# Weight terms of two output projections: formed on POOL in SBUF, or by adding transfers in DRAM

## The reference

```
y = concat([ya, yb, ym]) * silu(z)        # 512 x 1024
x = x + y @ w_out                         # w_out: 1024 x 1024, float32
```

## Time and profile before

| | us |
|---|---|
| median of 3 runs | 1134.42 |
| lowest and highest run | 1134.27, 1134.92 |
| profiled execution, its own time | 1134.12 |
| its span, first to last instruction | 1132.3 |
| PE busy | 1126.3 |
| DVE, ACT, POOL busy | 724.7, 614.6, 197.0 |

### The profile page before, as it was taken

One profiled execution on the slowest core, in us unless ns is written; L12 is line 12 of the kernel. 1 busy time (PEld: TensorE's weight loads), 2 busy tenths in 40 slices (PEclk: granted clock), 3 DMA queues, 4 the chain that ended last, 5 costly groups with the idle time before them and its releaser, 6 DMA issues.

```text
span 1132.3 us, 15715 instructions
## 1 busy us (share of the span) xinstructions
PE 1126.3 (99%) x6090; PEld 935.0 (83%) x6090; DVE 724.7 (64%) x1222; ACT 614.6 (54%) x1062; POOL 197.0 (17%) x193
## 2 busy tenths in 40 slices
PE   9999999999999999999999999999999999999998
PEld 7888888888888888888889888777888888877877
DVE  5584534599845776534558667667786575666786
ACT  5533431243436676634246677777545587577752
POOL 1000135440000000000000002643503000706530
PEclk9999999999999999999999999999999999999999
DMA  6423476673331212233255523231254233222431
GB/s 195 133 75 112 124 247 233 218 244 100 122 112 57 93 58 73 76 127 112 75 204 156 130 86 76 74 92 58 95 186 132 76 111 104 75 75 76 147 124 74
DMA packets 115026, 134.13 MB, mean 118 GB/s; under 512 B 18620, under 2 KB 93756, under 8 KB 113416
## 3 DMA queue, kind: packets, MB, share of 16 engines
q1 hardware_dynamic: 113720, 128.93, 35.9%
q10 hardware_dynamic: 1232, 4.19, 1.0%
HBM read 120.37 MB, written 12.74 MB: 118 GB/s over the span
## 4 chain that ended last, share of the span: by engine, by line
PE 98%; ACT 1%; DMA 0%; DVE 0%; issue 0%; DVEq 0%; ACTq 0%
PE acc L2052 22%; PE acc L2053 22%; PE acc L2054 22%; PE aux L2052 3%; PE aux L2054 3%; PE aux L2053 3%; PE aux L2538 3%; PE aux L2526 3%; PE acc L2502 3%; PE acc L2451 2%; PE acc L2453 2%; PE acc L2452 2%; PE aux L2284 1%; PE aux L2286 1%; PE aux L2285 1%; PE aux L2144 1%
## 5 line engine op out<-in xcount | busy, mean ns | idle before, releaser
L2052 PE MATMUL acc<-ht_hi,whi 128*128 128x512 f32 x712 | 278.1, 391 | 0.0
L2054 PE MATMUL acc<-ht_hi,wlo 128*128 128x512 f32 x712 | 277.1, 389 | 0.0
L2053 PE MATMUL acc<-ht_lo,whi 128*128 128x512 f32 x712 | 277.1, 389 | 0.0
L1406 DVE TENSOR_TENSOR wlo<-raw,whi 128x2048 fp32r<-128x2048 f32 x68 | 159.5, 2346 | 101.8 <-ACT whi L951 95.6
L951 ACT ACTIVATE whi<-raw 128x2048 fp32r<-128x2048 f32 x68 | 129.9, 1910 | 56.8 <-DMA raw<-w_in_dram 22.1
L2052 PEld LDWEIGHTS acc<-ht_hi,whi 128*128 128x128 f32 x712 | 133.7, 188 | 28.1 <-DVE wlo L1406 0.6
L2054 PEld LDWEIGHTS acc<-ht_hi,wlo 128*128 128x128 f32 x712 | 133.6, 188 | 27.9
L2053 PEld LDWEIGHTS acc<-ht_lo,whi 128*128 128x128 f32 x712 | 133.7, 188 | 27.1
L848 POOL TENSOR_SCALAR whi<-raw 128x512 fp32r<-128x512 f32 x52 | 39.5, 760 | 621.9 <-DMA raw<-e_w_in_dram 464.6
L2052 PE MATMUL acc<-whi,ht_hi 128*128 128x512 f32 (+1 forms) x224 | 83.9, 375 | 0.0
L2054 PE MATMUL acc<-whi,ht_lo 128*128 128x512 f32 (+1 forms) x224 | 83.8, 374 | 0.0
(11 more groups left out here) (344 smaller groups left out, 2160.5 us busy)
## 6 DMA issues: line engine op xcount, KB each, us to landing
raw<-w_in_dram SPq DMA_DIRECT2D x72, 512.0 KB, 4.6
raw<-o_w_in_dram SPq DMA_DIRECT2D x28, 512.0 KB, 4.7
weight_terms<-term_parts SPq DMA_DIRECT2D x8, 1024.0 KB, 4.8
raw<-e_w_in_dram SPq DMA_DIRECT2D x14, 512.0 KB, 5.2
raw<-w_proj_pool_dram SPq DMA_DIRECT2D x8, 512.0 KB, 4.0
term_parts<-o_w_out_dram SPq DMA_DIRECT2D x8, 512.0 KB, 6.4
raw<-w_proj_mlstm_dram SPq DMA_DIRECT2D x8, 512.0 KB, 4.1
raw<-w_out_dram SPq DMA_DIRECT2D x8, 512.0 KB, 4.4
```

The lines of the kernel that those rows point to most:

```text
L1406: v.tensor_tensor(wlo[:, slot, :], raw[:, slot, :], whi[:, slot, :].bitcast(F32), ALU.subtract).then_inc(w_split, 1)
L2052: mm(out_, w_hi_, x_hi, start=first, stop=False)
L2053: mm(out_, w_hi_, x_lo, start=False, stop=False)
L2054: return mm(out_, w_lo_, x_hi, start=False, stop=last)
```

## The change

The strips, POOL's subtractions and SP's 27 DMAs for them are gone, with the buffer `term_parts`. In their place POOL issues DMAs from DRAM to DRAM: 14 for the first layer and 8 for the second. For each layer four blocks are copied into the terms' places, two blocks are added to two of them, then T1 is added to T2, and T2 to T4; a wait stands between the steps. POOL begins once the eighth tile of transposed x is split (`tr_lo`). SP no longer does anything for the terms between weight loads, and waits for the last add (`fourth_added`) where it waited for the stores. The terms are now sums without a minus sign; the signs are taken up by the half sums and by the additions into the rows.

```diff
-            between_loads(0)
-            for u in range(4):
-                load(wview(A["w_proj_pool"][0]), u * UC, plan["pa"][0] + u)
-                between_loads(1 + u)
+            stage("pa", wview(A["w_proj_pool"][0]), 0)
...
                 load(W1, u * UC + COL_QK, plan["qk"][0] + u)
-                between_loads(5 + u)
...
-                    for landed in terms_out:
-                        sp.wait_ge(landed, 8 * len(BATCHES))
+                    sp.wait_ge(fourth_added, 32)
...
-            for b in range(len(BATCHES)):
-                pool.wait_ge(parts_in[b % 2], 16 * sum(PARTS[b % 2:b + 1:2]))
-                b11, b12, b21, b22 = (term_parts[:, b % 2, q, :] for q in range(4))
-                step(nc.gpsimd.tensor_tensor(b11, b12, b11, ALU.subtract))
-                step(nc.gpsimd.tensor_tensor(b12, b22, b12, ALU.subtract))
-                step(nc.gpsimd.tensor_tensor(b22, b22, b11, ALU.subtract))
-                nc.gpsimd.tensor_tensor(b21, b21, b22, ALU.subtract).then_inc(terms_made, 1)
+            def block(L, row, col):
+
+                view, cols = wview(A["eo"[L] + "_w_out_2"][0]), slice(WIDE * col, WIDE * col + WIDE)
+                if L or row:
+                    return [(slice(0, P), slice(0, 4), view[:, 4 * row:4 * row + 4, cols])]
+                halves_ = A["e_w_out_2"][0][0:3 * P].rearrange("(e k p) n -> e p k n", e=2, p=HD2)
+                return [(slice(HD2 * e, HD2 * e + HD2), slice(0, 3), halves_[e, :, :, cols]) for e in range(2)] + \
+                    [(slice(0, P), slice(3, 4), view[:, 3:4, cols])]
+
+            def weight_sums(L):
+                copied = blocks_copied_of(L)
+                for q, (row, col) in ((T1, (0, 0)), (T3, (0, 1)), (T2, (1, 1)), (T4, (1, 0))):
+                    for rows, ks, view in block(L, row, col):
+                        pool.dma_start(terms_dram[L, q][rows, ks, :], view).then_inc(blocks_copied, 16)
+                pool.wait_ge(blocks_copied, copied)
+                for q, (row, col) in ((T1, (0, 1)), (T3, (1, 1))):
+                    for rows, ks, view in block(L, row, col):
+                        pool.dma_start(terms_dram[L, q][rows, ks, :], view, accum_op=ALU.add).then_inc(pairs_added, 16)
+                pool.wait_ge(pairs_added, pairs_added_of(L))
+                pool.dma_start(terms_dram[L, T2], terms_dram[L, T1], accum_op=ALU.add, max_dma_last_dim=4 * WIDE).then_inc(third_added, 16)
+                pool.wait_ge(third_added, 16 * (L + 1))
+                pool.dma_start(terms_dram[L, T4], terms_dram[L, T2], accum_op=ALU.add, max_dma_last_dim=4 * WIDE).then_inc(fourth_added, 16)
...
+            for L in range(2):
+                if L == 0:
+                    pool.wait_ge(tr_lo, KT)
+                weight_sums(L)
...
-                        ins = v.tensor_tensor(sum_raw[:, k, :], y_tile(L, k)[:, UC:S], y_tile(L, k + 4)[:, UC:S], ALU.add)
+                        ins = v.tensor_tensor(sum_raw[:, k, :], y_tile(L, k + 4)[:, UC:S], y_tile(L, k)[:, UC:S], ALU.subtract)
...
-                        ins = v.tensor_tensor(sum_less[L][:, k, :], sum_raw[:, k, :], y_tile(L, k)[:, 0:UC], ALU.subtract)
+                        ins = v.scalar_tensor_tensor(sum_less[L][:, k, :], sum_raw[:, k, :], -1.0, y_tile(L, k)[:, 0:UC],
+                                                     ALU.mult, ALU.subtract)
...
-                    return v.tensor_tensor(rows, bank, rows, ALU.add)
+                    return v.tensor_tensor(rows, rows, bank, ALU.subtract if half else ALU.add)
...
-                        ins = v.tensor_tensor(sum_less[L][:, k, :], y_tile(L, k + 4)[:, 0:UC], sum_less[L][:, k, :], ALU.subtract)
+                        ins = v.scalar_tensor_tensor(sum_less[L][:, k, :], y_tile(L, k + 4)[:, 0:UC], -1.0, sum_less[L][:, k, :],
+                                                     ALU.mult, ALU.subtract)
```

More of the change, by code:

```diff
@@ L223, in hybrid_block_then_two_attention_layers @@
         w_late = at("w_late", [P, SLOT], HT + 16 * K)
-        term_parts = at("term_parts", [P, 2, 4, WIDE], R0)
         memT_o = [at("memT_o_hi", [P, KT, MEM], OP + 16 * K, F32R), at("memT_o_lo", [P, KT, MEM], OP + 24 * K, F32R)]
@@ L342, in hybrid_block_then_two_attention_layers @@
         mixed_in = sem("w_mixed_in")
-        parts_in = [sem(f"term_parts_in{i}") for i in range(2)]
-        terms_made = sem("terms_by_pool")
-        terms_out = [sem(f"terms_stored{i}") for i in range(2)]
+        blocks_copied = sem("weight_blocks_copied")
+        pairs_added = sem("weight_pairs_added")
+        third_added = sem("weight_third_block_added")
+        fourth_added = sem("weight_fourth_block_added")
         term_ready = sem("term_ready")
@@ L377, in hybrid_block_then_two_attention_layers @@
         X_READS, TERMS, LATE = 6, 10, 4
-        BATCHES = [(L, k) for L in range(2) for k in range(4)]
-        PARTS = [3 if L == 0 and k < 3 else 2 for L, k in BATCHES]
         A11_B11, S3_T3, A12_B21, S2_T2, S1_T1, S4_B22, A22_T4 = range(7)
@@ L888, in _, with blocks_copied_of, pairs_added_of @@
+            def blocks_copied_of(L):
+                return 16 * 8 + 16 * 4 * L
+            def pairs_added_of(L):
+                return 16 * 4 + 16 * 2 * L
+            for L in range(2):
+                if L == 0:
+                    pool.wait_ge(tr_lo, KT)
+                weight_sums(L)
             for u in range(4):
```

## The result

Eight executions of the changed kernel took from 1135.43 to 1140.84 us, with a median of 1140.0. Eight of the kernel before, beside them, had a median of 1134.47. The ratio is 1.004, with an interval from 1.003 to 1.005: slower, by 5.5 us or 0.4%. The prediction was 1134.4 with a range up to 1138.5, and is wrong.

What follows compares the result with a forecast made beforehand. TensorE, busy 1126.3 of 1132.3 us, was taken as the bound. Terms summed to 0 on its work and waits, so the forecast was the old median, about 1134.4 us; likeliest 1133.9 to 1135.5, range up to 1138.5.

Steps and rivals of the forecast that it cites:

- The same DMAs as traffic: Terms' transfers moved into the stretch from 17.7 us, beside weight loads: a unit 0 to 4 us later, cost 0.
- upper bound of 6.6: Most that a weight unit could land later beside the terms' transfers: 6.6 us, three times 3.3 us at 316 GB/s.
- The spare time: Weight load issued at 40.59, due at ACT at 51.97: 4.7 us to spare after landing by 47.3.
- The nearest row: Old kernel's DMA engines from 140 to 160 us: 0.79 busy with no PE wait, taken as grounds for cost 0.
- the second rival: Weights late behind adding transfers: four units each 1.9 us late, 7.6 us, 1142; decided by landing about 11 us after issue; 9%.
- two turns' bytes: Upper-bound assumption on DMA sharing: the terms' 2 KB rows get two turns' bytes for each 1 KB of weights.
- The first rival: DVE slowed by POOL's issuing at 65 to 76 us, factor 1.43: TensorE stops 4.8 us, 1139.2; 11%.
- The switch at 84 us: Weight-unit switch without spare time: split ends at 83.78, weight load at 83.84 waited 0.18 us; later DVE paid in full.
- SP's and POOL's old work: POOL's 32 subtractions and SP's 19 loads and 8 stores removed: TensorE waited for none, so worth 0.
- the signs cost nothing: DVE in the output stages and additions into rows: 0.1 us a layer against 3.1 us to the next deadline, cost 0.
- The terms, forecast to stand between 95 and 325 us: Both layers' DRAM-to-DRAM transfers from 17.7 us take 77 to 307 us; slack over 400 us before use, cost 0.
- at most 66: Work taken from POOL: 32 tensor_tensor subtractions at 2.1 us, together at most 66 us, worth 0 to TensorE.

Runs made afterwards that it cites:

- run 6: The changed kernel, with POOL waiting until each copy has landed before issuing the next; adds and start unchanged: 1133.86 us, ratio 0.9996.
- run 3: The kernel before with only the signs moved: POOL adds instead of subtracting, DVE's four places as in the change; no transfers moved: 1134.33 us, ratio 0.9999.
- run 2: The changed kernel with POOL's transfers set to start later, at about 118 us instead of 17.7: 1134.24 us, ratio 0.9998.
- run 8: The changed kernel with copies in place of the adds, same number, size and order of transfers, so its terms are no sums: 1135.3 us, ratio 1.0009.

## Why the prediction was wrong

*The step that failed* is "The same DMAs as traffic", with its "I take 0 to 4, under the spare time". What a unit came later by was 9.6 us for the load it looked at (15.8 against 6.2 in the profile of 1140.88) and 12.5 for the one before it (17.9 against 5.4 in that of 1136.08). Even the upper bound of 6.6 was under both. The spare time was right: 9.6 less the 4.7 us is 4.9, and ACT stood for 4.80. Two choices made the term too small.

- *The nearest row was not near.* The stretch from 140 to 160 us with 0.79 busy and no wait was the reason for taking 0. There the strips came a few at a time and SP, which also issues the weights, issued them. The change queues eight transfers at once. The run with copies one at a time (0.67 busy, nothing lost) is like that old row, and the changed kernel (0.98) is not. The depth was named under the second rival, and then priced out with the same row.
- *The bound gave the terms two turns' bytes.* The records show about one packet of each queue for one of the other: 443 beside 420 above, and 454 beside 420 from 30 to 36 us. The page of the profile gives the mean time of a packet: 0.063 x 1134.2 us x 16 engines / 6496 = 176 ns in POOL's queue, 0.316 x 1134.2 x 16 / 107144 = 54 ns for one of 1 KB in SP's. If an engine served both one for one, 1 KB of weights would pass every 230 ns, 16 engines would carry 71 GB/s, and a unit of 1.05 MB would take 14.7 us instead of 3.3. That is an estimate from these means and counts; it comes near the landings of a unit's second half, 15.8 and 17.9 us after its issue. It supposes that packets of the other queue are waiting for the whole 14.7 us, as they were with eight copies queued (443 beside 420) and were not with one (115 beside 957, run 6). How an engine chooses between the queues no run here shows; only the counts are measured.

The load at 19.27 was not looked at either. The prediction took the landing of one load, that at 40.59, for the stretch, and the transfers start at 17.7.

*TensorE's clock* is in no step. The price of a late unit was taken to be its wait. A wait of 3.8 us cost another 2.8 for the clock, in the profile of 1140.88. Its mean clock, 0.997, is the lowest in the group (three of the ten have it); how much of the 5.5 us of the median the clock has, at 0.998 to 0.999, isn't measured.

*The second rival*, weights late behind the adding transfers, was the right mechanism, at 9% and 1142. Its place and its deciding point (a landing about 11 us after issue) held. Its price came near for another reason: it counted four units of 1.9 us each, where one unit of 3.8 us and the clock did it. *The first rival*, DVE slowed by POOL's issuing, did not happen. Line 1398 in the changed kernel, with POOL issuing beside it from 18 to 120 us (duration ns min/median/max):

```profile
L1398 DVE TENSOR_TENSOR wlo<-raw,whi x68: 2281/2291/2294, 21.5 to 970.0; 128x2048 fp32r<-128x2048 f32 x68
```

The longest is 2294 ns, where POOL's subtractions had made it 3277. The switch at 84 us with nothing to spare added nothing. DVE was rightly priced as unharmed by POOL's issuing.

*The steps that held.* SP's and POOL's old work was worth nothing to TensorE beyond the 0.3 us above; the signs cost nothing (run 3). The terms, forecast to stand between 95 and 325 us, stand some 10 us after 118.89. POOL's busy time fell by 31.9 us; with the 19.3 us of its 22 issues added, 51 us of subtractions went, inside the "at most 66". The DMA share rose from the first slices on, as said.

*What stays open.* A half clock was seen in two profiles of the 1140 us kind, one of them of the changed kernel. For the other executions only the mean clock is known. It is 0.997 or 0.998 in six of the ten of the upper group and 0.999 in four. A mean of 0.999 proves little by itself: one execution of the lower group has it (1135.43), and so has the profiled one of run 2, at 1134.28 us, where TensorE loses nothing. Which of the two loads suffers is taken from one profile each: the start of the adds at 38.64 or 40.89 against a load at 40.6 goes with it, but no run fixed that alone.

## What to carry to other kernels

Before moving bulk transfers into a stretch, ask how many of them will be in flight at once when the next needed load is issued. Estimate that load's landing one packet for one (packet time of one queue plus packet time of the other) for as many packets as the other queue has waiting, not by free bandwidth: here that gives 14.7 us, where 15.8 and 17.9 were measured, and the bounds by bandwidth had given 6.6 us of delay at most, where it was 9.6 and 12.5. Here one wait per transfer kept the same bytes, in the same place, off the critical path. Look up the spare time of every load in the stretch, follow what stands behind the late one in ACT's and DVE's programs, and price a stop of TensorE of several microseconds with the clock that it may lose, not with its length alone: after the stops of 3.80 and 4.17 us here the half clock cost another 2.8 and 1.6 us.

## What the hardware showed that was not expected

- An adding packet of POOL's queue took about as long as a copying one with twice the bytes: 177 ns for 1980 bytes and 173 ns for 3.8 KB (run 8). Over the whole execution it was 6.3% of the engines for 6496 packets (176 ns each, 2583 bytes on average) with the adds, 4.2% for 4448 (171 ns, 3772 bytes) with copies in their place.
- TensorE stood for 3.80 and 4.17 us and ran at a granted clock of 0.50 after it, for 6 and about 3 us, which cost 2.8 and 1.6 us. In the second the clock had fallen 0.2 us before TensorE started again, in the first 0.9 us before. After stops of 0.84, 1.02 and 1.3 us the granted clock of the profiled executions stayed at 1.00.
- In the changed kernel POOL's issue of one transfer took 0.55 to 0.88 us for a first-layer copy and 1.0 us or more for an add, and DVE's splits beside it kept their 2.29 us.
- Two DRAM-to-DRAM phases of the same size differ by half in time: the four adds took 18 us, the four copies in their place 12.

```profile
weight_terms<-o_w_out_dram POOLq DMA_DIRECT2D x6, 1024.0 KB, 14.9
weight_terms<-weight_terms POOLq DMA_DIRECT2D x4, 1024.0 KB, 9.3
```

These rows of the changed kernel's page (KB each, us to landing) are the price that no row of before could give for a 1 MB transfer from DRAM to DRAM: 14.9 us at the median when several are queued, 9.3 for the third and fourth adds, which had none of POOL's ahead of them.
